# Attention preparation: queries turned ahead of the last projection group, block scores and fox queries inside it, fox keys inside the attention core, squares on ScalarE

## The reference, cut to what matters

```python
proj = h @ w_in
qa, kc, vc, ksl, vsl, kwn, vwn, ga, qb, kb, vb, fb = _split(proj, A_SPLITS)
qa = partial_rope(rmsnorm(heads(qa, NSA_HEADS), nsa_q_norm), cos, sin)
...
k_cmp = partial_rope(rmsnorm(compress(kc, pe_k, ck1, ck2), nsa_k_norm), ccos, csin)
...
s_c = jnp.einsum('bqgrd,bngd->bgrqn', qg, k_cmp) * scale      # block scores, n = 15 blocks
p_c = masked_softmax(s_c, cmp_end[None, :] <= tq[:, None])
o_c = jnp.einsum('bgrqn,bngd->bqgrd', p_c.astype(v_cmp.dtype), v_cmp)
...
qb = rmsnorm(heads(qb, FOX_HEADS), fox_q_norm)
kb = rmsnorm(heads(kb, FOX_HEADS), fox_k_norm)
s_f = (jnp.einsum('bqhd,bkhd->bhqk', q, kb) * scale + cq[..., None] - cum_t[:, :, None, :])
```

## Time and profile before

| | |
|---|---|
| runs | 1255.34, 1254.10, 1254.38 us; median 1254.38 |
| profiled execution | 1254.76 us, of which the span of the instructions is 1252.7 us |
| PE busy | 1227.2 us, 98% of the span |
| DVE, ACT, POOL busy | 982.8 (78%), 807.0 (64%), 56.2 us (4%) |
| stretch that the change touches | from about 34 us to 146 us of the span |

### The profile page before, as it was taken

One profiled execution on the slowest core, in us unless ns is written; L12 is line 12 of the kernel. 1 busy time (PEld: TensorE's weight loads), 2 busy tenths in 40 slices (PEclk: granted clock), 3 DMA queues, 4 the chain that ended last, 5 costly groups with the idle time before them and its releaser, 6 DMA issues.

```text
span 1252.7 us, 16095 instructions
## 1 busy us (share of the span) xinstructions
PE 1227.2 (98%) x6001; PEld 1020.3 (81%) x6007; DVE 982.8 (78%) x939; ACT 807.0 (64%) x870; POOL 56.2 (4%) x52
## 2 busy tenths in 40 slices
PE   6999999999999999999999999999999999999997
PEld 5888888888889887888888888888888888888886
DVE  4977654455466667999889889889889989989896
ACT  5445454334446455777777777777777777777773
POOL 1130000000000011010000000000000000000300
PEclk9999999999999999999999999999999999999999
DMA  9640054445544434999999999999999999999992
GB/s 372 239 168 1 2 201 172 173 172 189 202 168 146 143 135 149 364 393 379 394 385 367 396 387 368 393 385 368 397 379 369 399 380 368 390 374 369 397 421 86
DMA packets 52136, 361.42 MB, mean 289 GB/s; under 512 B 5824, under 2 KB 6080, under 8 KB 9824
## 3 DMA queue, kind: packets, MB, share of 16 engines
q1 hardware_dynamic: 49008, 349.41, 72.2%
q0 software_dynamic: 3056, 11.02, 2.2%
HBM read 354.63 MB, written 5.77 MB: 288 GB/s over the span
## 4 chain that ended last, share of the span: by engine, by line
PE 94%; DVE 3%; ACT 2%; issue 1%; POOL 0%; DMA 0%; another core or an unknown queue 0%; SPq 0%; DVEq 0%; ACTq 0%
PE bank L548 28%; PE bank L550 28%; PE bank L549 28%; PE bank L1040 2%; PE bank L765 1%; PE bank L737 1%; PE bank L899 1%; DVE low L1437 1%; PE bank L747 1%; PE bank L558 1%; ACT hT_hi L1146 1%; PE bank L1005 0%; ACT whi L1131 0%; PE bank L713 0%; PE bank L700 0%
## 5 line engine op out<-in xcount | busy, mean ns | idle before, releaser
L1981 DVE TENSOR_TENSOR low<-raw,whi 128x2048 fp32r<-128x2048 f32 x260 | 594.8, 2291 | 66.3 <-ACT whi L1371 59.3
L1371 ACT CAST whi<-raw 128x2048 fp32r<-128x2048 f32 x260 | 497.2, 1912 | 114.4 <-PE bank L550 113.9
L548 PE MATMUL bank<-whi,hT_hi 128*128 128x512 f32 (+1 forms) x1104 | 431.4, 391 | 7.9 <-DVE low L1437 7.0
L550 PE MATMUL bank<-whi,hT_lo 128*128 128x512 f32 (+1 forms) x1104 | 429.6, 389 | 0.0
L549 PE MATMUL bank<-low,hT_hi 128*128 128x512 f32 (+1 forms) x1104 | 429.0, 389 | 0.0
L548 PEld LDWEIGHTS bank<-whi,hT_hi 128*128 128x128 f32 x1104 | 207.8, 188 | 50.9 <-issue 7.3
L550 PEld LDWEIGHTS bank<-whi,hT_lo 128*128 128x128 f32 x1104 | 207.8, 188 | 42.9
L549 PEld LDWEIGHTS bank<-low,hT_hi 128*128 128x128 f32 x1104 | 207.9, 188 | 41.9
L1437 DVE TENSOR_TENSOR low<-raw,whi 128x2048 fp32r<-128x2048 f32 x69 | 157.7, 2289 | 47.1 <-ACT whi L1131 47.0
L548 PE MATMUL bank<-whi,h_hi 128*128 128x512 f32 x440 | 181.2, 412 | 0.0
L550 PE MATMUL bank<-whi,h_lo 128*128 128x512 f32 x440 | 172.6, 392 | 0.0
(11 more groups left out here) (298 smaller groups left out, 837.2 us busy)
## 6 DMA issues: line engine op xcount, KB each, us to landing
raw<-in_weights SPq DMA_DIRECT2D x329, 1024.0 KB, 5.3
sums<-ybuf POOLq DMA_DIRECT2D x7, 512.0 KB, 7.0
arena<-in_compress SPq DMA_DIRECT2D x1, 1088.0 KB, 13.8
x<-in_x SPq DMA_DIRECT2D x2, 512.0 KB, 5.8
tokens<-hng POOLq DMA_DIRECT2D x2, 512.0 KB, 3.4
out<-x SPq DMA_DIRECT2D x4, 256.0 KB, 2.7
cst<-in_constants SPq DMA_DIRECT2D x1, 601.0 KB, 10.8
picks<-in_norm_row POOLq DMA_DIRECT2D x1, 512.0 KB, 3.7
```

What stands on the lines that cost most here:

```text
L548: mm(out_, a_hi, b_hi, start=start, stop=False)
L550: return mm(out_, a_lo, b_hi, start=False, stop=stop)
L1371: nc.scalar.copy(whi[:, u % SPLIT, :, :], raw[:, u % RAW, :, :]).then_inc(S["w_hi"], 1)
L1981: V.tensor_tensor(low[:, u % RAW, :, :], raw[:, u % RAW, :, :], whi[:, u % SPLIT, :, :].bitcast(F32), ALU.subtract).then_inc(S["w_lo"], 1)
```

## The change

- PE: `cum` goes to bank 6 and, with the turning of the queries, ahead of group 5. Group 5 is now done row tile by row tile (`by_tile`): first rows 0 to 127 into bank 6, then rows 128 to 255 into bank 7, with work hooked in: the block scores after the fourth of the first eight steps, the turning of the fox queries between the tiles, the turning of the block probabilities after the sixth step of the second tile. The block values are multiplied between the first and the third unit's scores. The fox keys are turned in the core, four heads each after the turning of units 3, 5, 7 and 9, through bank 7.
- DVE loses the three large squares and one of two copies of the compressed inputs, and the copies of the turned keys, to ACT. The fox heads are multiplied by the root alone (L1542 of the new program); their gain is applied by ACT when it copies the turned heads out, as a scale per partition (a new column pair of the small table). The split of unit 14 moves behind the first two row maxima.
- ACT: squares of queries, fox queries and fox keys; order of its last copies adapted.
- The small table grows from 550 to 552 columns.

The diff, cut to its core:

```diff
@@ tensor engine @@
-            def by_tile(u0, cg, banks, turn=None, hook_at=None, hook=None):
+            def by_tile(u0, cg, banks, turn=None, hooks={}, first="tile0"):
...
-            in_group(5)
+
+            pe.wait_ge(S["fox_lf"], 1)
+            pe.wait_ge(S["proj"], 8)
+            mm(bank[6][:, 0:8], tri, fz[:, 4, 0:8], start=True, stop=True)
...
             pe.wait_ge(S["head_done"], 2)
-            pe.wait_ge(S["vbd"], 1)
-            pe.wait_ge(S["kcmpT"], 1)
             for i in range(4):
                 t, half = i // 2, i % 2
                 if i < 2:
                     pe.wait_ge(S["headT"], i + 1)
+                elif i == 2:
+                    pe.wait_ge(S["vbd"], 1)
+                else:
+                    pe.wait_ge(S["kcmpT"], 1)
...
+            pe.wait_ge(S["aug"], 1)
+            by_tile(U_A_IN, 5, (6, 7), None, {(0, 4): block_scores, (1, 0): fox_queries, (1, 6): block_probs}, "vb_rows")
...
             qk(0)
             qk(1)
+            block_values()
             for u in range(AU):
                 if u + 2 < AU:
                     qk(u + 2)
                 turn(u)
+                if u in (3, 5, 7, 9):
+                    pe.wait_ge(S["proj"], 12)
+                    pe.wait_ge(S["foxT"], 4 + (u - 3) // 2)
+                    fox_turn(4 + (u - 3) // 2, 7)
                 if u >= 1:
                     pv(u - 1)
@@ scalar engine @@
+            def head_squares(cg, half):
+
+                act.wait_ge(S["proj"], 2 * cg + 2)
+                A(sq[:, half * 1024:half * 1024 + 1024].rearrange("p (t n) -> p t n", t=NT), proj[cg][:, :, :], ACT.Square)\
+                  .then_inc(S["head_sq"], 1)
...
+            for cg in range(A_IN_CG - 1):
                 split(2 * cg + 4)
...
                 if cg == 2:
+                    act.wait_ge(S["head_done"], 1)
+                    head_squares(2, 0)
+                if cg == 3:
+                    head_squares(3, 1)
+                if cg == 4:
+                    act.wait_ge(S["head_ss"], 2)
+                    head_squares(4, 0)
+                split(2 * cg + 5)
...
+            act.wait_ge(S["vb_rows"], 1)
+            rows_out(5, 0)
+            for i in range(4):
+                fox_out(i, i)
+            split(14)
+            act.wait_ge(S["units_used"], 12)
+            rows_out(5, 1)
@@ vector engine @@
-            dve.wait_ge(S["proj"], 8)
-            head_squares(fox(0), NH, 2, 3)
+            dve.wait_ge(S["head_sq"], 2)
+            head_sums(NH, 2, 1024)
             split(12)
+            fox_scale(0)
+
             dve.wait_ge(S["vrep"], 1)
...
-            fox_scale(0)
-            dve.wait_ge(S["proj"], 10)
-            head_squares(fox(1), NH, 3, 4)
...
+            dve.wait_ge(S["cum"], 1)
...
             rowmax(0)
             rowmax(1)
+            block_part(0)
+            block_part(1)
+            split(14)
```

More of the change, by code:

```diff
@@ L617, in by_tile @@
                     if t == 0:
-                        last.then_inc(S["tile0"], 1)
+                        last.then_inc(S[first], 1)
             pe.wait_ge(S["ident_in"], 16)
@@ L687, in _, with block_scores, fox_turn @@
                 last.then_inc(S["headT_psum"], 1)
[L689 to L705, removed]
+            def block_scores():
+                pe.wait_ge(S["proj"], 10)
+                pe.wait_ge(S["headT"], 6)
+                for t in range(NT):
+                    for h in range(NH):
+                        g = h // 4
+                        last = mm(bank[4][:, t * P + h * 16:t * P + h * 16 + NCMP], qT[0:HD, h, t * P:(t + 1) * P],
+                                  kcmpT[0:HD, g * NCMP:(g + 1) * NCMP], start=True, stop=True)
+                last.then_inc(S["cmp_s"], 1)
+            def fox_turn(i, b):
                 w, t, half = i // 4, i // 2 % 2, i % 2
@@ L1160, in _, with rows_out @@
             act.wait_ge(S["rstd"], 1)
-            for cg in range(A_IN_CG):
+            def rows_out(cg, t):
+                w = FRONT_WIDTH.get(cg, BLK)
+                A(proj[cg][:, t, 0:w], bank[4 + 2 * (cg % 2) + t][:, 0:w], ACT.Copy, scale=rstd[:, t:t + 1])\
+                  .then_inc(S["proj"], 1)
+            def head_squares(cg, half):
+                act.wait_ge(S["proj"], 2 * cg + 2)
+                A(sq[:, half * 1024:half * 1024 + 1024].rearrange("p (t n) -> p t n", t=NT), proj[cg][:, :, :], ACT.Square)\
+                  .then_inc(S["head_sq"], 1)
@@ L1162, in _, with fox_out @@
+            def fox_out(i, b):
+                w, t, half = i // 4, i // 2 % 2, i % 2
+                act.wait_ge(S["foxT_psum"], i + 1)
+                A((fqT, fkT)[w][0:66, half * 4:half * 4 + 4, t * P:(t + 1) * P],
+                  bank[b][0:66, :].rearrange("p (h n) -> p h n", h=4), ACT.Copy,
+                  scale=sml[0:66, R_FCOL + w:R_FCOL + w + 1]).then_inc(S["foxT"], 1)
+            for cg in range(A_IN_CG - 1):
                 split(2 * cg + 4)
-                w = FRONT_WIDTH.get(cg, BLK)
@@ L1164, in _ @@
                 act.wait_ge(S["units_used"], 2 * (cg + 1))
                 for t in range(NT):
-                    A(proj[cg][:, t, 0:w], bank[4 + 2 * (cg % 2) + t][:, 0:w], ACT.Copy, scale=rstd[:, t:t + 1])\
-                      .then_inc(S["proj"], 1)
-                if cg < A_IN_CG - 1:
-                    split(2 * cg + 5)
-                if cg == 2:
+                    rows_out(cg, t)
+                if cg == 1:
+                    act.wait_ge(S["kc_psum"], 2)
+                    src = bank[1][0:HD, :].rearrange("p (g n) -> p g n", g=NG)
+                    nc.scalar.copy(kc2[0:HD, 1, :, :], src).then_inc(S["kc"], 1)
+                    nc.scalar.copy(kc2[HD:P, 1, :, 0:SEQ - 1], src[:, :, 1:SEQ]).then_inc(S["kc"], 1)
@@ new lines, in _ @@
+                if cg == 2:
+                    act.wait_ge(S["head_done"], 1)
[6 more added lines that the diff above has]
+                split(2 * cg + 5)
+                if cg == 2:
+                    for t in range(NT):
+                        act.wait_ge(S["headT_psum"], t + 1)
+                        nc.scalar.copy(keyT[0:HD, :, t * P:(t + 1) * P],
+                                       bank[t][0:HD, :].rearrange("p (h n) -> p h n", h=4)).then_inc(S["headT"], 1)
@@ L1642, in heads, with block_part @@
                 return ap.rearrange("p (h d) -> p h d", h=NH)
[L1644 removed]
+            def block_part(t):
                 dve.wait_ge(S["cmp_o"], t + 1)
@@ L2105, in layout @@
     small[:, R_A1:R_A1 + NK * 16] = cw[:, 3072:3088].reshape(NK, P, 16).transpose(1, 0, 2).reshape(P, -1)
+    small[HD:HD + 2, R_FCOL:R_FCOL + 2] = 1.0
+    for v, name in enumerate(("a_fox_q_norm", "a_fox_k_norm")):
+        small[0:HD, R_FCOL + v] = a(inp[name])[0]
     for v, name in enumerate(("a_pe_k", "a_pe_v")):
```

161 lines of the change are left out of this document (81 added, 80 removed).

## The result

The changed kernel takes 1264.21 us (median of six; the four undisturbed executions 1262.43 to 1264.33, median 1264.07), the kernel before 1254.79 us in the same session (1254.10 to 1255.44): ratio 1.0074, interval 1.0062 to 1.0087, by the undisturbed ones. It is slower by 9.3 to 9.4 us, where 1.3 us and a range up to 1258.6 had been forecast. Two further executions, 1289.83 and 1291.06 us, are left out of that comparison; what they most likely are comes up in the second set of experiments.

The account below looks back on a forecast made before the run. PE between projection and core was taken as the bound. 5.7 us won, 5.4 lost and 1.6 for one clock fall gave +1.3 us, 1256.0 on the profiled execution, 1255.6 as median; range 1252.3 to 1258.6 us.

Parts of the forecast that it names:

- What bounds the kernel: PE, busy 98%, between projection and core; the new order can win at most 5.2 us there.
- Part 1: Squares and copies moved to ACT: DVE delivers 4.2 us earlier at first, mostly eaten again; `vbd` at 79.3 us.
- Part 2: Queries and `cum` ahead of group 5: new 3.1 us wait for `vbd`, group 5 starts at 80.3, 5.5 us later.
- Part 3: Work inside group 5: 16.5 us to the core's first scores, at 96.8 instead of 102.53, 5.7 us won.
- Part 4: Work entering the core: values, fox keys, a 1.7 us wait and ACT's copies lengthen it, 5.4 us lost.
- The sum at full clock: From group 5 through the core: 5.7 us won against 5.4 us lost, -0.3 us.
- Part 5: PE's clock around group 5: one half-level fall, half of 3.4 us, +1.6; bounds 0 and 3.4 us once more.
- Two falls: Rival: the wait ahead of group 5 and the block scores each lower the clock, 3.4 us, 1257.5 us; chance 0.20.
- No fall: Rival: clock stays up over the wait ahead of group 5, -0.3 us, 1254.1 us; chance 0.22.
- The gain comes through: Rival: the core hides fox keys and the split, 3.9 us, giving 1250.1 us without a fall; chance 0.06.
- DVE later: Rival: queries' turning held by `vbd`, DVE later by another split, 2.3 us, giving 1257.9 us; chance 0.10.
- a half level longer than 6.8 us: Sign of being wrong: PE's half-clock stretch, expected somewhere between 78 and 92 us, lasts longer than 6.8 us.

Follow-up runs that it names:

- second set of experiments: One session of follow-ups, kernel before at 1254.38 us (25 executions); includes kernel before with only split 14 moved into the core: 1255.84 to 1256.66 or 1286.03 to 1290.78 us.
- second experiment: Changed kernel with `vbd` and the block keys' copy formed on DVE ahead of the fox query scaling: median 1258.24 us, in groups; profiled execution 1251.47 us.
- fifth experiment: Changed kernel with filler products in both waits and block scores spread over four steps of group 5: 1257.33 us, ratio 1.0017; profiled execution 1253.99 us.
- last experiment: Kernel before with fillers ahead of and among the block scores, 2.0 us in all: 1256.53 us, ratio 1.0015; one execution 1252.94 us.
- sixth experiment: Kernel before with only split 14 moved behind the core's second row maximum: four executions 1255.84 to 1256.66 us, eight 1286.03 to 1290.78 us.
- three sets: The sessions in which all follow-up kernels ran; the kernel before took 1254.44 (31 executions), 1254.38 (25) and 1254.05 us (27) in them.
- fourth: Changed kernel with `vbd` and key copy ahead of fox scaling, split 14 behind the third row maximum, block scores spread over four steps: 1253.63 us, ratio 0.9993.
- eighth: The fourth experiment's kernel with five filler products ahead of group 5, in the wait for the forget gates' products: 1254.03 us, ratio 0.9993.
- first: Changed kernel with 13 filler products before the wait for `vbd` and 7 before the core's first value products: 1254.47 us, ratio 1.0002.

## Why the prediction was wrong, step by step

**What bounds the kernel:** right. PE between 74 us and the core's end carries all of the loss; of the 10.2 us that the core ends later, the span (1262.1 against 1252.7) keeps 9.4.

**Part 1** held to 0.4 us in every time: rotation's end 66.1 (66.08 measured), split until 69.2 (69.06), sum ends 72.1 (71.83), root 77.4 (77.09), `vbd` 79.3 (78.96). POOL's first step was caught behind the split again, 2.17 us; the rule of the Trainium skill, "SBUF — State Buffer", section "Who interferes with whom", that a VectorE instruction with two SBUF inputs contends with a GpSimd instruction that reads SBUF, agrees with this trace as with the one before: the split runs from 71.75 us, POOL's step from 71.92.

**Part 2:** the wait for `vbd` was put at 3.1 us and measured 2.60; group 5 at 80.3, measured 80.58. **Part 3:** from group 5 to the core's first scores 16.5 us; 16.96 in the second experiment's trace, at full clock. **Part 4:** a core longer by 5.4 us. In the fifth experiment's trace, at full clock, it runs from 97.00 to 145.50, 48.50 us, against 43.13 from 102.53 to 145.66: 5.4. Of it the wait on split 14 was put at 1.7 us, measured 1.55. The sum at full clock, -0.3 us, is -0.16 at the core's end of that trace and -0.2 cleared as above, closer than traces that drift by over 1 us can promise; the four executions of the fifth experiment that kept the level, 1253.77 us in the mean, are 0.6 below the 1254.38 of before. The step order, the queues and the durations were read rightly.

**Part 5, the clock,** is the step that failed: one fall at 1.6 us was taken, and the runs show three that cost 10.5 us together. It went wrong in four places:

- *How many falls.* One was taken, two were a rival with a chance of 0.20. There were three. The prediction looked for thin stretches among the products that the change moves, the wait for `vbd` and the block scores, and found both. It did not put the question to its own part 4: there a wait of 1.7 us enters the core, whose products are small (turned probabilities, 64 value columns), and the sum took it by its length alone. That the core of before is at the full level throughout is no evidence for one with such a wait: its own was 0.4 us.
- *What one costs.* One fall of 6.8 us costs at most 3.4 by part 5's own working; 1.6 was taken. The kernel before's own, in the last experiment, is worth 3.6, by one execution; here the two ahead of the core cost 5.6 us, the one inside it 5.0. And "once more 3.4" for two falls together does not follow from its rows: two of the old length can cost 6.8 us, and 1254.4 - 0.3 + 6.8 is 1260.9, above the range.
- *How long one lasts.* 6.8 us, the length in the old trace, was taken as the length of any. The one in the core lasted 10.2 us, and 75.1 us in the sixth experiment. "Half of the 3.4, since the low level will partly lie over work that waits anyway" holds for the first of the three alone, whose first 1.6 us are the end of the wait.
- *The upper end.* The bound "3.4 us, once more" came from the one fall that the trace showed, so every case that the range took in had at most two falls.

What the three cost follows from the traces. Ahead of the core are 13.6 us at the half level: from the block values' first product to the core's first scores it is 28.30 us (74.06 to 102.36), against 23.64 in the fifth experiment (73.36 to 97.00), of which 0.9 is the spreading, so 5.6 us. In the core are 10.2 us, and its length is 53.46 instead of 48.50, 5.0 us. Together 10.5 us. With the -0.2 at full clock this is the 10.3 us by which the way from the block values to the core's end is longer than before (81.76 against 71.47).

A rule bears on the size: the Trainium skill, "TensorE: Matmul & The Clock Gate", section "Terms", puts the penalty of time at the lower level at that time multiplied by the part of the clock that is missing; for 23.8 us at half the clock that is an estimate of 11.9. The traces have 10.5; the first 1.6 us of the first stretch are the end of PE's wait for `vbd`.

**The rivals.** "Two falls" had the right mechanism and side, and names the right places for two of the three. "No fall" (1254.1) and the sum behind it are borne out by the fifth experiment's executions at full clock (1253.77 in the mean). "The gain comes through" did not occur: the core did not hide the fox keys. "DVE later" did not occur. Of the listed signs of being wrong, "a half level longer than 6.8 us" is the one that came.

## What to carry to other kernels

When an edit puts a wait of one or two microseconds among small matrix products, count the clock as well as the wait: here waits of 1.1 to 1.6 us went with losses of 2 to over 30 us. Ask it of every place where the edit adds a wait or gathers small products, also in a stretch that has always been at full level, and take as the upper end that each of them falls, at the full price. Read the single executions with their mean granted clock before comparing medians: groups of times with different clocks are one program with and without a fall.

## What the runs showed of the hardware

**A fall can last much longer than what stands before it.** With PE busy for 10.2 of 10.2 us, and for 74.11 of 75.1 us, the level stayed at the half, on products that ran at the full level in the kernel before. What ended the long one is open; the level came back some 7 us behind the core's end, within the output projection. The Trainium skill, "TensorE: Matmul & The Clock Gate", section "Seeing it yourself", tells of the clock having been seen stuck at a quarter for over 50 us, and warns that such records have been unreliable. Here the level is the half, and the products bear it out: eight value products take 1.81 us in the long stretch, 1.10 just before it.

**The same order falls or doesn't.** Four kernels above all (second, fourth, fifth and eighth) show groups of executions 2 to 9 us apart whose mean clocks differ by 0.003 to 0.007, beside the long falls. What decides is not visible in their traces, since the profiled execution is one of them; why the kernel before is steady (its 83 executions beside the three sets lie within 2.8 us) while these are not stays open too.

**Neither a wait nor small products decide alone, and fillers don't hold the level surely.** The level fell with hardly any idle time before it (first and eighth experiment: PE busy for 7.40 of 7.40 and 5.75 of 5.80 us), and it stayed up over a wait of 1.6 us (second). Twenty products in two waits gave back 9.7 us. Five in the wait of 1.3 us changed nothing, and twelve around and between the block scores of 15 columns did not prevent the fall in ten of eleven executions of the kernel before.
